# A layer loop rotated: the next layer's first halves during the last gate chunk, first loads at other times, y copied by two engines

## What is computed

```python
for li in range(2):                              # trunk_layer
    h = rms_norm(x, g_mix)
    A, B, C, D = split(h @ w_in)                 # four head groups, each its own attention
    x = x + concat(attn_A, attn_B, attn_C, attn_D) @ w_out
    x = x + square(relu(rms_norm(x, g_mlp) @ w_up)) @ w_down
    x = x + (ple @ w_ple) * sigmoid(rms_norm(x, g_ple) @ w_ple_gate)
return y_prompt, y_sample, and the new cache rows
```

## Time and profile before

| | us |
|---|---|
| runs before (3) | 3452.08, 3455.05, 3459.05; median 3455.05 |
| profiled execution, its own time | 3460.97 |
| its span | 3459.2 |
| PE busy | 3334.7 (96%) |
| PE weight loads busy | 3017.2 (87%) |
| POOL busy | 2259.8 (65%) |
| DVE, ACT busy | 1241.1 (36%), 1162.8 (34%) |
| mean DMA rate | 131 GB/s |
| mean granted TensorE clock | 0.977 of full |

### The profile page before, as it was taken

The page is one execution under the profiler, slowest core; times in us unless marked ns, Lnnn a source line. Parts: engine busy times, 40 slices in busy tenths (PEclk is TensorE's granted clock), DMA queues, the critical chain, the costliest instruction groups (busy, mean ns, idle before and its releaser), DMA issues.

```text
span 3459.2 us, 60576 instructions
## 1 busy us (share of the span) xinstructions
PE 3334.7 (96%) x20676; PEld 3017.2 (87%) x20676; DVE 1241.1 (36%) x2237; ACT 1162.8 (34%) x1686; POOL 2259.8 (65%) x2989
## 2 busy tenths in 40 slices
PE   7999999999999999999989999989999999999998
PEld 5777766699999999999967776668999999999998
DVE  4335454452041240323252444536412403204143
ACT  3334232333333333334343332314333333233342
POOL 5654200298898888888766550005988988888885
PEclk9999999999999999999999999989999999999999
DMA  5443322245555455554454433223555554554544
GB/s 156 130 118 111 112 66 82 84 135 152 153 152 152 144 150 153 149 155 142 142 154 117 126 86 111 72 74 99 149 155 148 152 153 141 152 152 147 153 140 122
DMA packets 295726, 453.09 MB, mean 131 GB/s; under 512 B 36336, under 2 KB 111344, under 8 KB 294832
## 3 DMA queue, kind: packets, MB, share of 16 engines
q1 hardware_dynamic: 295328, 448.66, 44.2%
q0 software_dynamic: 144, 0.87, 0.1%
HBM read 435.54 MB, written 14.06 MB: 130 GB/s over the span
## 4 chain that ended last, share of the span: by engine, by line
PE 88%; issue 4%; DVE 3%; ACT 2%; DMA 1%; POOL 1%; SPq 0%; DVEq 0%; POOLq 0%; ACTq 0%
PE ps L706 20%; PE ps L707 20%; PE ps L705 19%; PE ps L803 5%; PE ps L766 5%; PE ps L791 5%; PE ps L769 4%; PE ps L768 3%; PE ps L895 2%; PE ps L899 1%; DMA ring<-in_w_in 1%; PE ps L841 1%; PE ps L930 1%; PE ps L898 1%; POOL wlo L668 1%
## 5 line engine op out<-in xcount | busy, mean ns | idle before, releaser
L668 POOL TENSOR_TENSOR wlo<-ring,whi 128x256 fp32r<-128x256 f32 x2400 | 1832.7, 798 | 833.0 <-ACT whi L1142 832.9
L1142 ACT ACTIVATE whi<-ring 128x1024 fp32r<-128x1024 f32 x600 | 636.3, 1062 | 1346.6 <-PE ps L707 1339.8
L705 PE MATMUL ps<-xhi,wlo 128*128 128x320 f32 x2560 | 792.3, 310 | 13.8 <-POOL wlo L668 9.5
L706 PE MATMUL ps<-xlo,whi 128*128 128x320 f32 x2560 | 795.3, 311 | 0.0
L707 PE MATMUL ps<-xhi,whi 128*128 128x320 f32 x2560 | 791.8, 309 | 0.0
L707 PE MATMUL ps<-hhi,whi 128*128 128x320 f32 x2176 | 674.0, 310 | 0.0
L705 PE MATMUL ps<-hhi,wlo 128*128 128x320 f32 x2176 | 661.3, 304 | 0.0
L654 POOL TENSOR_TENSOR rlo<-ring,whi 128x256 fp32r<-128x256 f32 (+2 forms) x576 | 423.4, 769 | 321.5 <-ACT whi L1126 321.1
L706 PE MATMUL ps<-hlo,whi 128*128 128x320 f32 x2048 | 629.9, 308 | 0.0
L705 PEld LDWEIGHTS ps<-xhi,wlo 128*128 128x128 f32 x2560 | 485.2, 190 | 17.0 <-issue 15.2
L706 PEld LDWEIGHTS ps<-xlo,whi 128*128 128x128 f32 x2560 | 483.5, 189 | 0.8
(11 more groups left out here) (246 smaller groups left out, 3152.2 us busy)
## 6 DMA issues: line engine op xcount, KB each, us to landing
ring<-in_w_up SPq DMA_DIRECT2D x256, 512.0 KB, 3.7
ring<-in_w_down SPq DMA_DIRECT2D x256, 512.0 KB, 3.8
ring<-in_w_in SPq DMA_DIRECT2D x120, 512.0 KB, 3.7
ring<-in_w_out SPq DMA_DIRECT2D x64, 512.0 KB, 3.9
ring<-in_w_ple_gate SPq DMA_DIRECT2D x64, 512.0 KB, 3.8
xsave<-x SPq DMA_DIRECT2D x8, 640.0 KB, 5.6
x<-xsave SPq DMA_DIRECT2D x8, 640.0 KB, 4.6
ring<-in_w_in SPq DMA_DIRECT2D x16, 288.0 KB, 2.9
```

Source lines behind the costliest of these rows:

```text
L668: last = nc.gpsimd.tensor_tensor(wlo[:, s, c:c + LO_COLS], ring[:, s, c:c + LO_COLS], whi[:, s, c:c + LO_COLS].bitcast(f32), ALU.subtract)
L705: mm(out, lo[:, k, cols], xh, start=start, stop=False)
L706: mm(out, hi[:, k, cols], xl, start=False, stop=False)
L1142: A(whi[:, s, :], ring[:, s, :], ACT.Copy).then_inc(hi_ready, 1)
```

## The change

The order of the work around the layer boundary, the start and the end changes; what is computed does not.

- x_prompt is loaded into `xin`, which lies where `xhi` is, instead of into `hid`. g_mix and the first two units (`EARLY = 2`) are loaded ahead of the loop; PE gives the ring free at its very start.
- At the end of a layer SP loads the next layer's first two units (after the last layer layer 0's, unused), and g_mix of the next layer is loaded behind the embeddings.
- ACT scales blocks 0 to 11 (`EARLY_X = 12`) and makes the halves of units 0 and 1 ahead of the loop, and for the next layer between the last conversions of the gate and `sigmoids(l, 3)`. The loop starts with halves of unit 2, blocks 12 to 15, halves of unit 3.
- DVE splits blocks 0 to 3 (`EARLY_LO = 4`) between the copies of x at the start, and for the next layer before block 12 of the gate.
- PE starts group A when three of the four gate chunks are finished; chunk 0 now sits in banks 0 to 2, chunk 1 in banks 5 to 7 and waits for the fourth. Chunk 2 waits for the copies of chunk 1.
- `first_loads` is cut in five parts, ahead of units 5 to 9.
- y: the first four tiles are those whose blocks are final after three gate chunks or lie in q = 0 and 1; ACT copies seven tiles and DVE five.

```diff
+        xin = sb("xin", [128, 2, DM], at=at)
...
+        EARLY, EARLY_X, EARLY_LO = 2, 12, 4
+        Y_TILES = [(0, 0), (1, 0), (2, 0), (0, 1), (0, 2), (0, 3), (1, 1), (1, 2), (1, 3), (2, 1), (2, 2), (2, 3)]
+        Y_ON = "AAAADADADDAD"
...
-            return 0 if no == 1 else 5
+            return 0 if no == 0 else 5
...
             def beside(l, i):
-                if i == RING:
-                    first_loads(l)
+                if RING < i <= RING + 5:
+                    first_loads(l, i - RING - 1)
...                                                    # SP
+            load_mix(0)
+            for i in range(EARLY):
+                load_w_in(0, i, 0)
             with sp.Fori(0, DEPTH) as l:
                 hold(job_out, l * 8 + 1)
...
                         if n == RING:
                             load_embeddings(l)
+                            sp.wait_ge(xsplit, l * KB + KB)
+                            load_mix(l * -1 + (DEPTH - 1))
...
+                for i in range(EARLY):
+                    load_w_in(l + 1, i, l * -1 + (DEPTH - 1))
...                                                    # PE
-                    hold(proj_copied, 3 * (l * N_WIN + (0 if no == 2 else no - 1)) + t + 1)
+                    hold(proj_copied, 3 * (l * N_WIN + no - 1) + t + 1)
+                if (no, u, t) == (1, 0, 0):
+                    hold(half_free, l * CHUNKS + 2)
...
+            pe.sem_inc(unit_used, RING)
             hold(table_loaded, 16)
...
-            pe.sem_inc(unit_used, RING)
             with pe.Fori(0, DEPTH) as l:
-                hold(half_free, l * CHUNKS + 2)
+                hold(half_free, l * CHUNKS + 1)
...
-            hold(half_free, DEPTH * CHUNKS + 2)
-            for i in range(12):
-                t, q = i // 4, i % 4
+            for i, (t, q) in enumerate(Y_TILES):
+                if i == 0:
+                    hold(half_free, DEPTH * CHUNKS + 1)
+                if i == 4:
+                    hold(half_free, DEPTH * CHUNKS + 2)
                 if i >= 8:
-                    hold(y_copied, i - 7)
+                    hold(y_copied["A"], i - 7)
...                                                    # ACT
+            act.wait_ge(mix_loaded, 16)
+            for b in range(EARLY_X):
+                if b == EARLY_LO:
+                    halves(0, range(EARLY))
+                act.wait_ge(x_copied, b + 2)
+                gain_blocks(0, b, b + 1)
             with act.Fori(0, DEPTH) as l:
-                act.wait_ge(mix_loaded, 16 * (l + 1))
-                gain_pass(l)
+                halves(l, (2,))
+                act.wait_ge(half_free, l * CHUNKS + 2)
+                gain_blocks(l, EARLY_X, KB)
+                halves(l, (3,))
...
+                act.wait_ge(mix_loaded, 16 * (l + 2))
+                act.wait_ge(half_free, (l + 1) * CHUNKS + 1)
+                gain_blocks(l + 1, 0, EARLY_X)
+                halves(l + 1, range(EARLY))
                 sigmoids(l, 3)
+            for i in range(len(Y_TILES)):
+                if Y_ON[i] == "A":
+                    act.wait_ge(y_full, i + 1)
+                    A(*y_tile(i), ACT.Copy).then_inc(y_copied["A"], 1)
...                                                    # DVE
+                if 9 <= k < 9 + EARLY_LO:
+                    first_split(0, k - 9, k - 8)
...
-                first_split(l)
+                first_split(l, EARLY_LO, KB)
...
+                    if (c, m) == (3, 0):
+                        first_split(l + 1, 0, EARLY_LO)
```

More of the change, by code:

```diff
@@ L575, in load_embeddings, with load_mix, load_w_in @@
                 sp.dma_start(otmp[0:DSEQ, 2, :], I["p_sample"][l, 0]).then_inc(ple_loaded, 16)
+            def load_mix(l):
+                with nc.allow_non_contiguous_dma("feature-major gains"):
+                    sp.dma_start(gains[:, 0, :], I["g_mix"][l, :].rearrange("(a p) -> p a", p=128)).then_inc(mix_loaded, 16)
+            def load_w_in(l, i, lw):
+                no, u = STREAM[i]
+                _, _, nk, ncol, c0 = CHUNK_AT[no]
+                first = {"A": W_A, "B": W_B, "C": W_C, "D": W_D}[GROUP_OF[no]]
+                src = I["w_in"][lw, u * nk * 128:(u + 1) * nk * 128, first + c0:first + c0 + ncol]
+                load(l, i // RING, i % RING, nk * ncol, src.rearrange("(a p) n -> p a n", p=128))
             for tile in range(2):
[L578 to L579 removed]
+                sp.dma_start(xin[:, tile, :], I["x_prompt"][0, tile * 128:(tile + 1) * 128, :]).then_inc(x_loaded, 16)
             sp.dma_start(arena[0:DSEQ, 0:DM], I["x_sample"][0, :, :]).then_inc(x_loaded, 16)
+            load_mix(0)
+            for i in range(EARLY):
+                load_w_in(0, i, 0)
             with sp.Fori(0, DEPTH) as l:
                 hold(job_out, l * 8 + 1)
[L583 to L584 removed]
                 for i, (no, u) in enumerate(STREAM):
+                    if i < EARLY:
+                        continue
                     beside(l, i)
@@ L597, in _ @@
                         continue
[L598 to L602, removed]
+                    load_w_in(l, i, l)
                 for c in range(4):
@@ L1073, in _, with y_tile @@
                 last.then_inc(y_full, 1)
+        def y_tile(i):
+            t, q = Y_TILES[i]
+            n = 128 if t < 2 else DSEQ
+            staged = hid[:, :, :].rearrange("p a b -> p (a b)") if t < 2 else arena
+            at = t * DM if t < 2 else 0
+            return staged[0:n, at + q * 512:at + (q + 1) * 512], ps[0:n, i % 8, :]
         def norm_views(name):
@@ L1346, in add, with first_split @@
                 return V.tensor_tensor(out, a, b, ALU.add)
-            def first_split(l):
+            def first_split(l, b0, b1):
                 dve.wait_ge(mix_loaded, 16 * (l + 1))
-                for b in range(KB):
+                for b in range(b0, b1):
                     dve.wait_ge(gained, l * KB + b + 1)
@@ L1699, in _ @@
                     last.then_inc(x_copied, 1)
-            last.then_inc(half_free, 2)
+                else:
+                    last.then_inc(half_free, 2)
+                if 9 <= k < 9 + EARLY_LO:
+                    first_split(0, k - 9, k - 8)
             dve.wait_ge(half_free, 2)
```

43 lines of the change are left out of this document (21 added, 22 removed).

## The result

| | before | after |
|---|---|---|
| median of 5 runs each, us | 3452.97 (3449.73 to 3459.05) | 3433.97 (3432.46 to 3438.77) |
| ratio, 95% interval | | 0.994 (0.9925 to 0.9954) |
| profiled execution, its span | 3459.2 | 3431.0 |
| PE busy | 3334.7 (96%) | 3319.9 (97%) |
| mean granted TensorE clock | 0.977 | 0.984 |

The change makes the kernel 19 us faster by the medians and 21 by the ratio; the forecast was 22.7 us and 3432.3. A second comparison with five more runs of the changed kernel gave 3430.35 against 3455.6, 25 us by the medians; by its ratio, 0.9935 (0.9921 to 0.9948), it is 22.

A forecast was written before the change was run, and what follows sets the result against it. PE, busy 96% of the span, was taken as the bound, leaving only its idle stretches and clock to win. Start 10.8, boundary 8.7 and end 3.2 sum to 22.7 us: 3455.05 - 22.7 = 3432.3, range 3424 to 3442.

The forecast's parts named there:

- Start: forecast 10.8: Start of the kernel: 3.9 us from an earlier PE start plus 7.8 from the small vectors, less 0.6 and 0.3.
- rival 2: Start: early weights share the DMA engines with x and delay it, price up to 5 us; 3436; chance 0.08.
- The new wait of 0.6: First layer's row sums: wait for squares that need unit 7's conversion first in ACT's order; 0.6 us, bounds 0 to 1.3.
- the loss of 0.3 at unit 9: Each layer: unit 9's load goes out late behind the last part of the small vectors; 0.3 us, bounds 0 and 1.3.
- Boundary: forecast 8.7: Layer boundary: row sums 9.75 us earlier, less 0.8 for DVE's splits and 0.3 for unit 9; bounds 5 and 11.
- ACT's old chain: Boundary: last sigmoid, loop return 3.29, table load 1.28, conversion 1.06, then POOL's 3.15; holds unit 2 until 1742.8.
- End: forecast 3.2: End: immediate transposes and copies by two engines, then bandwidth-bound stores, end the span 3.2 us earlier; bounds 1.5 and 4.5.
- Their 7.8 in the sum: Start, first layer: small vectors no longer ahead of unit 4, so 5.33 idle and 2.5 us behind it go.
- Code fetch at the boundary (1): Boundary: code fetch, not data, holds PE, so it gives 3 instead of 8.7 us; 3438; chance 0.17.
- More than forecast (3): Splits stay fast, ACT comes round sooner, the clock holds at the start: 28 us won, 3427; chance 0.12.
- gain not felt (4): Attention stages: the waits return where DVE and ACT pace PE; under 6.9 us stays, 3450; chance 0.04.
- The slower rival (5): Units 5 to 9 of each layer: vectors' small packets hold up weight units, landings reaching 9.7 us; 3465; chance 0.03.

## Why the prediction was right

**Start: forecast 10.8, measured 58.54 - 48.74 = 9.8.** PE's first unit starts at 30.58 (forecast 30.6), and the 5.33 are gone. x lands at 14.48 and 13.81 for 14.36 and 13.88, so the early weights do not delay it and rival 2 fails. The new wait of 0.6 had been put at the row sums, and the loss of 0.3 at unit 9. Neither is there; a wait of 1.3 for POOL stands before unit 7 instead. The step had named the squares as next late and looked for them in ACT's order; what they hold up is POOL, through DVE's additions.

**Boundary: forecast 8.7, measured 44.2 - 34.4 = 9.7.** The path was the forecast's. The first gap is 1.91 and 1.46, less than the 2.2 to 3.3, because PE came round its loop sooner; unit 2 starts 11.55 and 11.20 us after the last gate matmul's end (forecast 11.1), held by ACT's old chain and POOL behind it, as forecast. PE stopped there for 2.11 and 2.21, not for 1 to 1.4, because it had begun sooner. The row sums come 35.16 and 33.73 later (forecast 33 to 36, its sum 34.3 + 1.1). The splits of blocks 4 to 15 were sized well at first: 0.98 + 0.76 less overlap, 1.58 a block from 1731.18 on.

**End: forecast 3.2, measured 17.4 - 14.4 = 3.1.** ACT loads no table before its copies. The first store goes 5.1 us after the last matmul (3421.80 - 3416.67), formerly 7.8.

**The vectors.** Their 7.8 in the sum were near the truth for this change (6.1 at the start in the kernel with nothing else changed, with a new wait of 1.25 already off), but the account of them was not whole. Taken alone they win 6.1 at the start and lose 3.9 at the boundary; taken away they cost 120.9 - 97.5 = 23.4 us in the stages and 14 to 18 in the runs (0.9976 - 0.9935 and 0.9992 - 0.994), not 7.8. PE's earlier starts (4.1 and 9.8) run into the wait for unit 4 unless it is gone too. The forecast could add its terms only because all were in. Two parts were never run by themselves: the early loads and scalings at the start, and PE's start on other banks after three gate chunks. What they give is read off the rows.

**Rivals.** Code fetch at the boundary (1) would have left most of the 11.39; the gaps of 1.91 and 1.46 refute it. More than forecast (3) and gain not felt (4) don't fit 3434. The slower rival (5) did not happen in the changed kernel, but something like it showed when the vectors moved to a worse place.

**The clock.** At the boundary, after 1.91 and 2.11 idle the rows keep it, and after 2.21 in the second profile. In other kernels it fell after 2.23, and after 2.09 in the one without large sums (the gap ends at 1724.58; the granted clock from 1726 to 1728 is 0.50). The forecast had it held after 2.23 and lost at 3.41. PE and a window of the kernel with y by one engine, then a window of the one with the vectors three units later, behind a gap of 2.49 at 1740.07:

```profile
1730.16 0.76 PE L797 MATMUL ps<-rlo,xw 128*128 128x512 f32 x1 [2.23 <-POOL rlo L683]
...
1731.00:1733.00 2.00, 2.00 (x6) 1.51 (x6) 2.00 (x3) 1.27 (x2) 2.00 (x4) 0.50 0.72 216
```

```profile
1741.00:1743.00 2.00, 2.00 (x10) 1.65 (x10) 2.00 (x4) 1.71 (x3) 2.00 (x4) 1.00 0.00 0
```

So pauses of 2.09 and 2.23 us cost half the clock once each, and one of 2.49 did not; 2.32 did in the kernel with the sums in pieces and did not in the first profile with the vectors in one block. The Trainium skill (TensorE: Matmul & The Clock Gate, HAM oscillation) tells of a kernel whose waits for DMAs, longer than these, bring the slow clock back each time. At the boundary the rows agree for the long ones: every pause of 2.51 us and more lost it. Between 2.09 and 2.49 they show both. At the start rows and profile disagree: behind the 1.44 the matmuls from 30.58 on follow each other at 0.43 us for 0.23 later, the pace of half clock, while the window from 31 to 33 has the granted clock at 1.00. So there the slow pace is read from the rows.

**The whole.** The stages' 22.6 is the forecast's 22.7, while the two comparisons gave 19 and 25 by the medians and 21 and 22 by the ratios. That the sum meets the stages to 0.1 us is in part luck: the start gave 1.0 less than forecast and the boundary 1.0 more. The spread of the comparisons is within what the rest does, whose ten stretches of 2 us each no forecast of this change could call.

## What to carry to other kernels

Work started earlier is won only if the next wait behind it goes too: here one block of small loads ahead of unit 4 ate earlier starts of 4.1 and 9.8 us, while moving those loads alone won 1.8 us in the stages and some 5 in the runs. Before moving such loads, list what else the same queue must issue where they are to go. When one gap closes, read the timeline again at the next two, and compare the distance between fixed points of the stage, not the gap. And check the engine that a row names against the time at which the needed piece of work was done: before units 0 and 2 at the boundary the engine named had been ready for 4.0 and 1.8 us.

## What the runs showed of the hardware

- **POOL and DVE shut each other out.** A split on DVE that takes 0.47 us took 3.06 (the row at 1710.58 above): it started inside POOL's row of 16, and ended only when that row had, at 1713.35. In the other direction POOL's splits took 1.09 us for 0.71 beside DVE's large additions and 0.77 without them; cutting the additions in pieces didn't help. One by one, the splits of the row at 49.49 took 0.73 to 0.76, but for four that took 3.33, 1.97, 1.31 and 0.99, each a little longer than the addition beside it (3.12, 1.91, 1.23 and 0.91): POOL waits for one whole addition at a time. The Trainium skill (SBUF — State Buffer, SBUF: two separate sides) calls the pair of ports that both use an exclusive lock, held for the whole instruction. The rows agree that they exclude each other, and POOL's waits are of one instruction of DVE each. But the 2.6 us that DVE waited are nearly four of POOL's instructions, not one.
- **Coming round a hardware loop** took DVE 3.19 us, ACT 2.57 and a table load of 1.28, and PE 1.46 to 2.51. For the shorter ones, 1.79 at most, the rows mostly name nothing; for the longer ones they name POOL, whose unit 0 had been ready for 4 us and more (1721.04 for a start at 1725.05, 1720.28 for one at 1725.16).
- **Two paces at one clock.** 172 or 175 matmuls in 25 us with PE never idle, for some 100 us at a time; cause open.
- **Issuing can block.** SP's first four weight loads, queued behind x, held SP for 12.13 us. It cost nothing here, as PE asks for the next ones later:

```profile
3.02 12.13 SPq L467 DMA_DIRECT2D ring<-in_w_in  x4
```
